# The low part of three down slabs a layer, from an accumulating DMA onto ScalarE's negated high part

## The reference, cut to what matters

```python
def swiglu(x, w_gate, w_up, w_down):          # w_gate, w_up: 1024 x 2816, w_down: 2816 x 1024
    return (jax.nn.silu(x @ w_gate) * (x @ w_up)) @ w_down
```

## Time and profile before

| | us |
|---|---|
| median of three runs | 1590.97 (1590.71 to 1591.17) |
| the profiled execution, its own time | 1590.62 |
| its span, first to last instruction | 1588.9 |
| PE busy | 1581.3 |
| DVE busy | 1138.0 |
| ACT busy | 831.8 |
| POOL busy | 35.5 |

### The profile page before, as it was taken

How to read it: one execution, slowest core, us unless ns; L and a number is a source line. 1 busy time by engine, 2 the same in 40 slices (tenths; PEclk the granted TensorE clock), 3 DMA queues, 4 the chain that set the end, 5 groups by cost and what they waited for, 6 DMA issues and landing times.

```text
span 1588.9 us, 21336 instructions
## 1 busy us (share of the span) xinstructions
PE 1581.3 (100%) x8746; PEld 1360.9 (86%) x8746; DVE 1138.0 (72%) x1384; ACT 831.8 (52%) x1125; POOL 35.5 (2%) x53
## 2 busy tenths in 40 slices
PE   9999999999999999999999999999999999999999
PEld 7888898878888888888899888889888888888887
DVE  6678856798767777768757677877766557766785
ACT  5555354775455535555444555556555436545552
POOL 0000000000000000000000000001000011000000
PEclk9999999999999999999999999999999999999999
DMA  9555684445566456655465655657565551056643
GB/s 308 187 197 187 198 270 151 137 139 180 164 206 226 171 199 196 192 183 213 158 225 176 196 185 172 236 176 250 175 188 199 187 199 58 25 167 193 193 154 117
DMA packets 228385, 291.23 MB, mean 183 GB/s; under 512 B 10628, under 2 KB 203840, under 8 KB 228160
## 3 DMA queue, kind: packets, MB, share of 16 engines
q1 hardware_dynamic: 228016, 289.61, 55.0%
q10 hardware_dynamic: 272, 0.26, 0.0%
HBM read 288.78 MB, written 1.05 MB: 182 GB/s over the span
## 4 chain that ended last, share of the span: by engine, by line
PE 95%; DVE 3%; ACT 1%; DMA 0%; POOL 0%; issue 0%; SPq 0%; DVEq 0%
PE bank L2204 24%; PE bank L2209 13%; PE bank L1990 7%; PE bank L1995 7%; PE bank L1999 7%; PE bank L2081 6%; PE bank L2073 6%; PE bank L2068 6%; PE bank L2042 2%; PE bank L2049 2%; PE bank L2044 2%; PE bank L2322 1%; PE bank L2319 1%; PE bank L2317 1%; PE bank L2640 1%; PE bank L1960 1%
## 5 line engine op out<-in xcount | busy, mean ns | idle before, releaser
L1230 DVE TENSOR_TENSOR w_lo<-raw,w_hi 128x2048 fp32r<-128x2048 f32 (+1 forms) x281 | 623.8, 2245 | 93.5 <-ACT w_hi L779 90.4
L779 ACT ACTIVATE w_hi<-raw 128x2048 fp32r<-128x2048 f32 (+1 forms) x280 | 524.8, 1884 | 155.4 <-DVE raw L1218 52.9
L2204 PE MATMUL bank<-xT,w_hi 128*128 128x512 f32 x1664 | 397.3, 391 | 0.0
L2204 PEld LDWEIGHTS bank<-xT,w_hi 128*128 128x128 f32 x1664 | 306.2, 188 | 59.5
L2209 PEld LDWEIGHTS bank<-xT,w_lo 128*128 128x128 f32 x1664 | 213.3, 191 | 8.1
L2209 PE MATMUL bank<-xT,w_lo 128*128 128x256 f32 x1664 | 215.9, 283 | 0.0
L1161 ACT ACTIVATE silu<-bank 128x256 f32<-128x256 f32 x104 | 34.3, 381 | 193.6 <-PE bank L2209 193.6
L2068 PE MATMUL bank<-w_hi,xT 128*128 128x512 f32 (+2 forms) x448 | 117.7, 392 | 0.0
L2081 PE MATMUL bank<-w_lo,xT 128*128 128x512 f32 (+2 forms) x456 | 115.3, 384 | 0.1
L2073 PE MATMUL bank<-w_hi,xT 128*128 128x512 f32 (+2 forms) x448 | 114.4, 384 | 0.0
L1995 PE MATMUL bank<-w_hi,hT_lo 128*128 128x512 f32 x416 | 107.3, 390 | 0.0
(11 more groups left out here) (325 smaller groups left out, 1820.7 us busy)
## 6 DMA issues: line engine op xcount, KB each, us to landing
raw<-in_ffn_w_gate_up_dram SPq DMA_DIRECT2D x176, 512.0 KB, 4.8
raw<-in_ffn_w_down_dram SPq DMA_DIRECT2D x132, 512.0 KB, 4.1
raw<-in_w_in_dram SPq DMA_DIRECT2D x44, 512.0 KB, 4.9
raw<-in_ffn_w_gate_dram SPq DMA_DIRECT2D x42, 512.0 KB, 4.1
raw<-in_ffn_w_up_dram SPq DMA_DIRECT2D x42, 512.0 KB, 5.1
raw<-in_conv_w_in_dram SPq DMA_DIRECT2D x24, 512.0 KB, 4.7
raw<-in_kv_w_dram SPq DMA_DIRECT2D x12, 512.0 KB, 4.8
raw<-in_w_out_dram SPq DMA_DIRECT2D x8, 512.0 KB, 3.7
```

The costliest lines, as they stand in the source:

```text
L779: nc.scalar.activation(w_hi[:, slot, 0:width], raw[:, slot, 0:width], ACT.Copy).then_inc(high_ready, 1)
L1230: nc.vector.tensor_tensor(w_lo[:, slot, 0:width], raw[:, slot, 0:width], w_hi[:, slot, 0:width].bitcast(F32), ALU.subtract).then_inc(low_r ...
L2204: nc.tensor.matmul(o[:], hi[:, c, at], x, start=kh == 0 and c == 0, stop=False, skip_group_check=True)
```

## The change

A new table, `FETCH`, names the plain pairs d = 1, 2, 4 of layers 0, 3, 5 and 9, and d = 1, 2 of layer 2: 14 slabs. For such a slab the split on DVE is left out. In its place ACT, behind the high copy, waits for that copy and writes `-w_hi` to `w_lo` (it rounds `-raw` in the same way). POOL waits for that (`negated`) and issues a DMA that reads the same 1 MB of `w_down` from HBM a second time and adds it onto `w_lo`, so that `w_lo` becomes `raw - w_hi`. PE waits for the landing (`low_landed`, two semaphores in turn) in place of `low_ready`; for all other slabs it waits for `low_ready` at a count without the fetched ones.

```diff
+FETCH = {0: (1, 2, 4), 2: (1, 2), 3: (1, 2, 4), 5: (1, 2, 4), 9: (1, 2, 4)}
...
+        FETCHED = {down_slab(n, i): (n, d) for n in FETCH for i, d in enumerate(down_order(n)) if d in FETCH[n]}
+        fetched = sorted(FETCHED)
+
+        def lows_to(k):
+            return k + 1 - sum(m <= k for m in fetched)
...
+                if kind == FFN:
+                    down = ffn_weights(ffn_number[n])[2]
+                    for number, k in enumerate(fetched):
+                        layer, d = FETCHED[k]
+                        if layer == n:
+                            pool.wait_ge(negated, number + 1)
+                            if number > 1:
+                                pool.wait_ge(low_landed[number % 2], 16 * (number // 2))
+                            pool.dma_start(w_lo[:, k % SLOTS, :].rearrange("p (c n) -> p c n", c=2),
+                                           down[2 * d * P:(2 * d + 2) * P, :].rearrange("(c p) n -> p c n", p=P),
+                                           accum_op=ALU.add).then_inc(low_landed[number % 2], 16)
...
                 nc.scalar.activation(w_hi[:, slot, 0:width], raw[:, slot, 0:width], ACT.Copy).then_inc(high_ready, 1)
+                if k in FETCHED:
+                    act.wait_ge(high_ready, k + 1)
+                    nc.scalar.activation(w_lo[:, slot, :], raw[:, slot, :], ACT.Copy, scale=-1.0).then_inc(negated, 1)
...
-                if k >= TOTAL:
+                if k >= TOTAL or k in FETCHED:
                     return
...
+            def wait_low(k):
+
+                if k in FETCHED:
+                    number = fetched.index(k)
+                    pe.wait_ge(low_landed[number % 2], 16 * (number // 2 + 1))
+                else:
+                    pe.wait_ge(low_ready, lows_to(k))
...
                     if not known:
-                        pe.wait_ge(low_ready, k + 1)
+                        wait_low(k)
```

More of the change, by code:

```diff
@@ L305, in two_block_kernel @@
         b_sums = sem("b_sums")
+        negated = sem("negated")
+        low_landed = [sem(f"low_landed{i}") for i in range(2)]
         s_made = sem("s_made")
@@ L2319, in seven_products @@
                                 nc.tensor.matmul(o[:], x_lo, hi[:, at, :], start=False, stop=False, skip_group_check=True)
-                            pe.wait_ge(low_ready, slab + 1)
+                            wait_low(slab)
                             for o, (x_hi, _), at in group:
```

## The result

The changed kernel takes 1645.59 us (median of four, 1642.96 to 1646.81) against 1591.07 us (four runs of the kernel before, 1590.71 to 1591.20). The ratio is 1.0341, with a 95% interval of 1.0323 to 1.0359: 54.5 us slower. The direction was forecast; 1608 us was not, and the range of 1590 to 1635 us did not hold the time.

The account below looks back on a forecast made before the run. PE, busy 1581.3 of 1588.9 us, was taken as the bound; DVE relief and ACT copies counted 0. Waits of 3.5 us in four layers and 3.0 in layer 2 summed to 17.0 us, giving 1608.0 us, range 1590 to 1635.

Parts of the forecast that it names:

- The transfer at double price: On the DMA engines: the accumulating DMA reads two operands, so 5.6 us of the engines, 7.8 us alone to landing.
- the step that I had called the most likely to fail: On the DMA engines: the price of the second read, taken as 5.6 us in all against 2.8 if free.
- the forecast one: Down products: a double-priced transfer with PE waits of a few us a layer, 1596 to 1620 us, chance 0.46.
- every rival: DMA cheap as a load, 1590.5 to 1593.5 us (0.33); slow issue or transfer, 1621 to 1641 (0.18); DVE relief, 1587.0 (0.03).
- The first wait of each layer: PE's wait for a landed sum at a layer's first pair of fetched slabs: 3 us.
- the two ends worked out: First pair of slabs: PE waits 4.8 us if loads and fetch share evenly, 3.5 us if the fetch goes first.
- The issue: On POOL: issuing a DMA takes 0.4 us, between bounds of nearly nothing and 2.6 us.
- The lock on DVE: On POOL: an issue might run only when DVE pauses, with DVE runs of 8.90 us; by the skill's rule 0.
- The further waits: PE at the third fetch of layers 0, 3, 5 and 9: 0.5 us added for each.
- The slack that I counted: PE at the third fetch: the wait already suffered is slack, so only 0.5 us is added.
- far slower: Issue of 2.6 us or transfer three times a load: 6 to 10 us a layer, 1621 to 1641 us, chance 0.18.
- a triple price: On the DMA engines: the transfer takes three times the load, 8.4 us, if the addition also slows the stream.

Follow-up runs that it names:

- copy made twice: The kernel before, with ACT making the high copy of the 14 slabs twice and no fetch: 1591.26 us, ratio 1.0002.
- the kernel with the late pairs: The changed kernel with the fetch on pairs 6, 8 and 9 (layer 2: 8 and 9) in place of 1, 2 and 4: 1628.49 us, ratio 1.0236.
- the kept-busy runs: The changed kernel with 16 products by zeros before the wait in eight slabs: 1643.30 us; the same with one fetch a layer, of pair 1: 1610.68 us.

## Why the prediction was wrong in size

**What held.** PE was the bound, and DVE's subtractions, 29 us of busy time, hid behind it (the kernel without the DMA). ACT's copies cost nothing (copy made twice). The transfer at double price, 5.6 us of the engines, was measured at 5.5 in place and 5.9 alone; alone it landed in 8.4 us against 7.8. This was the step that I had called the most likely to fail. Of the mechanisms the forecast one was right, but the time lies beyond its 1596 to 1620 us and beyond those of every rival.

**Terms of the sum that were mis-sized.**
1. *The first wait of each layer.* 3 us taken, 20.1 / 5 = 4.0 measured. Of the two ends worked out, 4.8 us was the wait for the first fetch at an even share, 3.5 us one for the second if the first went ahead. The first came close: the landing was forecast for 150.2, and PE went on at 149.59. The second did not occur, since slab 28's load was hardly late. I took 3 us, below both, because a waiting PE thins the crowd. It cannot do so for the first fetch: both loads beside it are issued before PE waits. Taking a value outside one's own bounds was the mistake.
2. *The issue.* 0.4 us taken, 1.2 us measured; 0.8 us later each time. The lock on DVE was not seen: the longest issue is 1.34 us, though DVE was busy for at most 0.69 us during any of them. In the kernel with the late pairs three issues (780.57, 1065.41, 1604.11) fell in 1.2 us in which DVE was busy throughout with its subtraction, and they took 1.2 us as well.
3. *The further waits.* I gave the third fetch of a layer 0.5 us. It is waited for some 5 us in three of four layers, 36.0 - 20.1 = 15.9 us in all. The slack that I counted was real, as the kernel with pairs 1 and 4 shows; the step that failed is that the second fetch was left out of the sum for the third. In layer 0 it makes the third's load 2.3 us late and its transfer 3.6 us longer.
4. *The clock.* No term at all. Behind the waits PE ran for stretches at 1.2 GHz, 18 us of full clock. With fetches behind each other that is largely time in which a landing would be waited for anyway; with one a layer it is 11 us of 31. In the trace of before no idle time of PE was longer than 1.2 us, so it could not be read there, but a forecast of waits should have asked what follows them.

Summed, in us:

| term | predicted | measured |
|---|---|---|
| five first fetches | 15.0 | 20.1 |
| four third fetches | 2.0 | 15.9 |
| lost clock | 0 | 18.1 |
| sum (growth of the span) | 17.0 | 54.1 |

So the two terms that failed are the third fetch's wait and the clock; the first wait was mis-sized by a quarter. My "far slower" case gave 1621 to 1641 us by other mechanisms (a slow issue, a lock, a triple price), none of which was seen; that it lies nearer is no merit of it.

**Left open.** With the first fetch before it the third took 9.3 to 10.8 us; alone in its layer, and in three layers of the changed kernel, 12.6 to 13.9. What decides between the two is not shown. In layer 3 of the changed kernel it took 9.7 us with 61.0% of the engines, and landed as PE came to it; with PE kept busy the same one took 12.4 us with 42.5%, and was waited for. So that layer escaped narrowly. Nor was the share of the 54.5 us measured that each cause would have alone: they are not additive, as the kept-busy runs show.

## What to carry to other kernels

A transfer that is to be hidden must be added up with the transfers that run in the same stretch, on all 16 engines together, up to its deadline; its length alone and the mean share of the DMA engines (55% here) said little. Where loads are issued as slots come free, a late transfer delays the next load, which delays the next transfer, so the second one can pay for its successor without ever waiting itself. Where the bounding engine shows no wait for another in the trace, relief of that other gained nothing, though it was 72% busy.

## What the runs showed of the hardware

- An accumulating DMA of 1.05 MB took 5.9 us of the 16 DMA engines and landed in 8.4 us. With a cast and no addition it was 3.4 us of the engines and 5.2 to landing; plain, beside the last loads, 3.1 and 5.4. POOL's issue took 1.2 us with the addition and 0.7 to 0.9 without.
- A fetch and the loads beside it did not slow each other evenly. Two load pieces issued with it landed in 3.7 and 5.1 us (3.1 and 4.2 before); two issued 2 us later took 10.2 and 10.9 (3.8 and 4.8 before), and the fetch 12.1.
- With two fetches in flight, four pieces of the next layer's load took up to 22.3 us to land. In 163:179 of that kernel the fetches had most of the engines, with fewer but larger packets than the loads (packets, MB, share):

```profile
q0 software_dynamic: 595, 2.31, 73.5%
q1 hardware_dynamic: 817, 1.47, 29.1%
```

- The granted clock of PE fell for a stretch at the waits of the changed kernel. In layer 0, where PE was idle for 3.63 us, it was still 1.00 in 149:149.6 and 0.54 in 149.6:153, when work had come back. In layer 3, with 4.15 us of idle time, it fell while PE was still idle: 0.54 in 757.3:759.4, and 0.50 in the 4 us of work behind. With one fetch a layer this cost 11.3 us for five waits (1622.03 against 1610.68 us).
